# A hybrid decoder step on one core: q kept by feature in the delta rule, the output scaling put behind the next tile's masks, and the gate copy put ahead of the weight rounding

## The chip, the cores and the metric

The kernel runs on one core of one Trainium2 chip. The metric is the time of one execution on the device in microseconds (us), given as the median of three runs. The engines are TensorE (PE; its weight loads are listed as PEld), VectorE (DVE), ScalarE (ACT), GpSimd (POOL), and SyncE (SP), which issues the transfers.

## The reference, cut to what matters

One decoder layer for a prompt of 2048 tokens (16 meta tokens before it) and 8 running sequences of 4 tokens, model width 1024. Window attention and a gated delta rule work side by side, are merged by sigmoid gates, and a feed-forward block follows. The part that the change touches is the delta rule: 4 heads of 128, chunks of 64 tokens.

```
qb = _l2norm(heads(qb, DK)) * (DK ** -0.5)
kb = _l2norm(heads(kb, DK))

def _gated_delta_chunk(S, q, k, v, g, beta):
    gc = jnp.cumsum(g, axis=-1)
    decay = where(incl, exp(gc[..., :, None] - gc[..., None, :]), 0.0)
    kk = einsum('bhid,bhjd->bhij', k, k)
    a_mat = where(strict, beta[..., :, None] * decay * kk, 0.0) + eye(L)
    eg = exp(gc)
    rhs = beta[..., None] * (v - eg[..., None] * (k @ S))
    u = triangular_solve(a_mat, rhs, lower=True, unit_diagonal=True)
    qk = einsum('bhid,bhjd->bhij', q, k) * decay
    o = eg[..., None] * (q @ S) + qk @ u
    S_new = exp(gc[..., -1]) * S + einsum('bhjd,bhj,bhje->bhde', k, exp(gc[..., -1:] - gc), u)

# behind it, for each token and head:
y = o * rsqrt(mean(o * o) + EPS) * w * silu(z)
```

## The kernel before

The prompt is worked in four groups of 512 tokens, each of four tiles of 128 tokens (two chunks each). Group 1 has a fifth, small tile "S" of 48 columns ahead of them: the meta tokens and the 8 running sequences. A group goes through projections, a short convolution (`conv`, which leaves q, k and v by feature in `post`), the delta rule tile by tile, the `z` projection, the output projections and the feed-forward block. Each engine has its own program (`tensor`, `scalar`, `gpsimd`, `vector`) in an order written out by hand; semaphores join them, and each queue is worked in its order.

A tile of the delta rule, by TensorE: `delta_rows` turns k, q and v from feature-major into rows (banks 6, 2, 7) and spreads the cumulated decays into bank 4; VectorE scales the rows (`scaled`: kn, qn, qe, kb, kw, bv); TensorE turns kn, qn and qe back (`turned`), ScalarE copies them (`turned_copy`) to kTd, qT and a part of WQ; `delta_scores` makes k k^T and k q^T; `delta_args` (VectorE) and `delta_decays` (ScalarE) make the decay masks, `delta_masks` applies them and leaves X; five levels of small products (`PT`, `DT`) invert the triangle; then WU (W transposed and U), and for each of the two chunks a product with the state S (L1390), u, the state's increment (L1402), the output (L1407) and the update of S (L2535). `row_squares`, `row_sums_of` and `row_factors` make the norms of the next tile's q and k; `delta_out` scales the output of the tile before.

In between, in numbered steps 0 to 17, `beside(t, k)` puts other work: quarters of the 16 gate products (`gate_quarter`, all in bank 0; in group 1 the last quarter of each gate is followed by 48-column products for the small tile) and the attention of the next tile (`attention_step`: inputs at step 2, scores at 3 and 8, softmax at 5 and 10, transposes at 6 and 11, values at 7 and 13). `QUARTERS` says how many quarters stand at each step; in groups 2 to 4 a gate ends at steps 2, 6, 12 and 17 of each tile. In group 1 a tile holds 11 quarters, so the ends fall elsewhere in each.

Weights come through SyncE's queue into `raw`; ScalarE rounds a unit (`weights_hi`, L617) and VectorE takes the rest (`weights_lo`, L624). A ring of three units holds both parts. When a gate j ends, `gate_logits` on ScalarE rounds the unit two ahead and then copies bank 0:

```
j = gate_k[0]
gate_k[0] += 1
hi_until("gate", j)
if first and j == 8:
    act.wait_ge(*made("state_out", 16))
act.wait_ge(*made("gate_ps", (j + 1) * (1 + F)))
...
act.copy(gate[:, j, MAIN], bank[0][:]).then_inc(sem("gate_e"), 1)
```

Of the kernel before, what the change touches and what calls it, by code (L numbers as in the profile page):

```python
# [59 lines left out]
assert sum(QUARTERS) * NT == 64 and QUARTERS_C + sum(QUARTERS_S) + sum(QUARTERS_0) * NT == 64  # L60
# [66 lines left out]
for _v, _names in {  # L127
# [28 lines left out]
            "osq_done rope_done",  # L156
# [23 lines left out]
            "bt_ps bt_rd nat_ps",  # L180
# [20 lines left out]
        (0, 30, 24):  # L201
# [7 lines left out]
        (0, 45, 36):  # L209
# [113 lines left out]
def program(nc, d):  # L323
# [422 lines left out]
    def group(g, first):  # L746
# [38 lines left out]
        quarters_of = lambda t: QUARTERS_S if t == "S" else QUARTERS_0 if first else QUARTERS  # L785
# [96 lines left out]
        def tensor(pe, claim):  # L882
# [263 lines left out]
            def rows_from(t, b, blk, v):  # L1146

                n = n_of(t)
                claim(b, "natq_done", v)
# [4 lines left out]
            def delta_values(t):  # L1154

                rows_from(t, 7 if first or t else 2, 2, 6 * ix[t] + 6)

            def delta_rows(t):
# [3 lines left out]
                rows_from(t, 6, 1, 6 * i + 5)  # L1162
                rows_from(t, 2, 0, 6 * i + 3)
                if first or t:
                    delta_values(t)
                claim(4, "arg_done", 2 * i + 2)
# [5 lines left out]
            def turned(t, q, b, src):  # L1172

                i, n = ix[t], n_of(t)
                pe.wait_ge(*made("natq_done", 6 * i + q + 1))
                claim(b, "bt_rd", 3 * i + q + 1)
                for x in range(NH):
                    last = nc.tensor.transpose(bank[b][:, n * x:n * (x + 1)], q4[src][0:n, x, :], c("ident")[0:n, 0:n])
                last.then_inc(sem("bt_ps"), 1)

            def delta_scores(t):

                i, w = ix[t], own_w(t)
                qT, kTd = q4["qT"], q4["kTd"]
                pe.wait_ge(*made("bt_rd", 3 * i + 1))
# [5 lines left out]
                pe.wait_ge(*made("bt_rd", 3 * i + 2))  # L1191
                claim(2, "QK_done", i + 1)
                for x in range(NH):
                    for cs in chunks(t):
                        last = nc.tensor.matmul(bank[2][cs, w * x:w * (x + 1)], kTd[:, x, cs], qT[:, x, cs], start=True, stop=True)
                last.then_inc(sem("kk_ps"), 1)

            def inside_conv(j):
# [7 lines left out]
                if not first and j == NCONV - 1:  # L1206
                    turned(0, 0, 1, "kn")
                    turned(0, 1, 3, "qn")
                    turned(0, 2, 5, "qe")
# [39 lines left out]
            def delta(t):  # L1249
                i, n, w = ix[t], n_of(t), own_w(t)  # L1250

                if first or t:
                    turned(t, 0, 1, "kn")
                    turned(t, 1, 3, "qn")
# [3 lines left out]
                if first or t:  # L1258
                    turned(t, 2, 5, "qe")
# [79 lines left out]
                if t == "S":  # L1339

                    pe.wait_ge(*made("WT_rd", 1))
                    pe.wait_ge(*made("bt_rd", 3))
                    claim(3, "small_done", 3)
                    for x in range(NH):
# [5 lines left out]
                        if x == 1:  # L1350
                            gate_quarter()
# [245 lines left out]
        def scalar(act):  # L1597
# [52 lines left out]
            def gate_logits():  # L1650
# [3 lines left out]
                hi_until("gate", j)  # L1654
# [52 lines left out]
            def turned_copy(t, q, b, dst):  # L1707

                n = n_of(t)
                act.wait_ge(*made("bt_ps", 3 * ix[t] + q + 1))  # L1710
                act.copy(WQ[:, :, CH:CH + n] if dst == "qeT" else q4[dst][:, :, 0:n], bank[b][:, 0:NH * n].rearrange("p (h n) -> p h n", h=NH)).then_inc(sem("bt_rd"), 1)

            def delta_decays(t):
# [6 lines left out]
                for x in range(NH):  # L1720
                    act.activation(q4["dA"][0:n, x, 0:w], q4["dA"][0:n, x, 0:w], ACT.Exp, scale=-1.0,
                                   bias=tg2[0:n, s, x:x + 1]).then_inc(sem("dec_done"), 1)
                for x in range(NH):
# [16 lines left out]
            for j in range(NCONV):  # L1740
# [4 lines left out]
                if not first and j == NCONV - 1:  # L1745
                    turned_copy(0, 0, 1, "kTd")
                    turned_copy(0, 1, 3, "qT")
# [1144 lines left out]
```

## Time and profile before

| what | value |
|---|---|
| median of three runs | 3335.37 us (3330.85 to 3346.25) |
| the profiled execution, its own time | 3332.55 us |
| its span, first to last instruction | 3330.7 us |
| mean granted TensorE clock | 0.990 |
| TensorE, VectorE, ScalarE, GpSimd busy | 97%, 60%, 46%, 12% of the span |
| delta rule of group 1, about | 162 to 453 us |

The page gives each engine's busy time; the timeline gives start, length, engine, line, operation, written and read tiles, a count where equal instructions are merged, and in brackets how long the engine had stood and what released it. The granted clock is 1.00 at full rate (2.4 GHz) and 0.50 at the lower level (1.2 GHz). Line numbers are those of the kernel before.

### The profile page before, as it was taken

How to read it: one execution, taken by the hardware profiler on the slowest of the kernel's cores; microseconds unless marked ns; L12 is line 12 of the kernel's file. 1: busy time of each engine (PE TensorE's matmuls, PEld its weight loads, DVE VectorE, ACT ScalarE, POOL GpSimd, SP SyncE). 2: the span in 40 equal slices, each digit the busy share in tenths (PEclk: the TensorE clock that was granted, in tenths of full speed). 3: DMA queues.
4: the chain of work that ended last, by engine and by line, in shares of the span. 5: the costliest groups of instructions: out<-in, count | busy, mean ns of one | idle time of the engine just before them, and what ended most of it. 6: DMA issues, size and time to landing. Idle time of an engine off the chain costs nothing. (4 is left out here: it accounts for less than half of the span.)

```text
span 3330.7 us, 59185 instructions
## 1 busy us (share of the span) xinstructions
PE 3247.1 (97%) x23574; PEld 2841.8 (85%) x23574; DVE 1986.5 (60%) x3721; ACT 1520.0 (46%) x3173; POOL 413.5 (12%) x453
## 2 busy tenths in 40 slices
PE   8999899999999999999999999999999999999998
PEld 7877789999998777898998777889998777789896
DVE  6645545543547654685766754587575855578484
ACT  5324443222235554464554654455454654446362
POOL 2211100432503111000003011000001211000000
PEclk9989999999999999999999999999999999999999
DMA  4211013655743111354553211345463211246463
GB/s 161 63 56 46 25 58 111 229 194 199 257 154 110 54 46 63 116 160 138 165 193 109 73 39 46 114 137 167 137 213 124 78 44 43 80 129 183 124 177 97
DMA packets 142816, 392.47 MB, mean 118 GB/s; under 512 B 18288, under 2 KB 20288, under 8 KB 139072
## 3 DMA queue, kind: packets, MB, share of 16 engines
q1 hardware_dynamic: 142544, 388.69, 36.5%
q8 instruction: 190, 3.11, 0.4%
q14 instruction: 82, 0.67, 0.1%
HBM read 353.95 MB, written 35.69 MB: 117 GB/s over the span
## 5 line engine op out<-in xcount | busy, mean ns | idle before, releaser
L624 DVE TENSOR_TENSOR wl<-raw,wh 128x512 fp32r<-128x512 f32 (+1 forms) x795 | 747.1, 947 | 573.2 <-ACT wh L617 569.6
L617 ACT CAST wh<-raw 128x512 fp32r<-128x512 f32 (+1 forms) x795 | 636.0, 808 | 459.6 <-PE bank L892 370.8
L892 PE MATMUL bank<-xnT,wh 128*128 128x512 f32 (+2 forms) x2432 | 725.3, 382 | 9.0 <-ACT gate L1663 7.3
L892 PE MATMUL bank<-hnT,wh 128*128 128x256 f32 (+2 forms) x3016 | 580.7, 290 | 3.1 <-ACT V L1959 3.1
L892 PEld LDWEIGHTS bank<-xnT,wh 128*128 128x128 f32 x2432 | 430.3, 192 | 81.6 <-issue 16.5
L892 PEld LDWEIGHTS bank<-hnT,wh 128*128 128x128 f32 x3016 | 473.6, 188 | 8.5 <-ACT V L1959 3.7
L892 PE MATMUL bank<-hid,wh 128*128 128x512 f32 (+1 forms) x1760 | 467.6, 353 | 0.0
L892 PE MATMUL bank<-xnT,wl 128*128 128x512 f32 (+2 forms) x1280 | 461.8, 365 | 0.0
L892 PE MATMUL bank<-hnT,wl 128*128 128x256 f32 (+2 forms) x1508 | 437.2, 290 | 0.0
L892 PE MATMUL bank<-Tm,wh 128*128 128x256 f32 x2016 | 368.7, 282 | 0.2 <-ACT sg L1959 0.2
L892 PEld LDWEIGHTS bank<-hid,wh 128*128 128x128 f32 x1760 | 309.5, 188 | 46.0 <-issue 0.3
L892 PEld LDWEIGHTS bank<-Tm,wh 128*128 128x128 f32 x2016 | 310.2, 189 | 1.0 <-ACT sg L1959 0.8
L892 PE MATMUL bank<-hid,wl 128*128 128x512 f32 (+1 forms) x880 | 311.0, 353 | 0.0
L892 PEld LDWEIGHTS bank<-hnT,wl 128*128 128x128 f32 x1508 | 283.6, 188 | 2.1
L892 PE MATMUL bank<-Tm,wl 128*128 128x256 f32 x1008 | 284.1, 282 | 0.0
L892 PEld LDWEIGHTS bank<-xnT,wl 128*128 128x128 f32 x1280 | 245.9, 192 | 41.2
L892 PEld LDWEIGHTS bank<-Tm,wl 128*128 128x128 f32 x1008 | 190.3, 189 | 0.0
L892 PEld LDWEIGHTS bank<-hid,wl 128*128 128x128 f32 x880 | 165.4, 188 | 23.8
L892 PE MATMUL bank<-mixT,wh 128*128 128x512 f32 (+1 forms) x640 | 170.7, 355 | 1.8 <-DVE mixT L2593 1.8
L892 PE MATMUL bank<-oT,wh 128*128 128x512 f32 (+1 forms) x640 | 169.5, 353 | 1.3 <-ACT sz L1897 1.3
L892 PEld LDWEIGHTS bank<-mixT,wh 128*128 128x128 f32 x640 | 113.9, 190 | 18.8 <-ACT mixT L1919 2.0
L2351 DVE SCALAR_TENSOR_TENSOR cy<-pre,pr,cy 128x512 f32<-128x512 f32 (+1 forms) x144 | 125.3, 870 | 5.1
(380 smaller groups left out, 4527.3 us busy)
## 6 DMA issues: line engine op xcount, KB each, us to landing
raw<-in_wstream SPq DMA_DIRECT2D x346, 512.0 KB, 3.5
raw<-wsum SPq DMA_DIRECT2D x252, 256.0 KB, 3.4
raw<-in_wstream SPq DMA_DIRECT2D x189, 256.0 KB, 2.8
ops_in<-in_wstream SPq DMA_DIRECT2D x44, 512.0 KB, 7.6
wsum<-ops_out SPq DMA_DIRECT2D x22, 1024.0 KB, 6.3
hT<-in_xT SPq DMA_DIRECT2D x4, 2048.0 KB, 8.9
out_yp_out<-hT SPq DMA_DIRECT2D x16, 512.0 KB, 3.0
xr<-in_x_prompt SPq DMA_DIRECT2D x12, 512.0 KB, 7.9
```

Source lines behind the costliest of these rows:

```text
L617: act.copy(hi_cell(n), raw_cell(n)).then_inc(sem("hi_done"), 1)
L624: nc.vector.tensor_tensor(lo_cell(n), raw_cell(n), hi_cell(n).bitcast(F32), ALU.subtract).then_inc(sem("lo_done"), 1)
L892: ins = nc.tensor.matmul(*a, **k)
L2351: ins = v_.scalar_tensor_tensor(out, src(i), w(i), out, ALU.mult, ALU.add)
```

## The change

q is no longer scaled as rows. The unscaled q stays by feature in `post`; the scores of q and k read it there, and the part of WQ for q is `post` times `eG`, the exponential of bank 4, which ScalarE makes in one instruction more (`dec_done` counts 10 a tile instead of 9). q's norm enters as a factor of the output instead: GpSimd multiplies the mean square by the square of the factor (slot 1 of `fac`) before the root and the root by the factor (slot 0) after it. q rows are still made for tiles 1 to 3, for their sums of squares. The norm's root for k is taken apart from the one for q.

The order changes as well. `delta_args` of the next tile stands at the end of a tile in every group; ScalarE does tile 0's `delta_decays` inside the small tile in group 1. `delta_out` of the tile before stands behind step 1. Rounding and subtraction of gate weights (`gate_weights`) come behind the gate copy, and at step 17 only behind the next tile's decays (ScalarE) and scaled rows (VectorE). In group 1 three quarters move out of the small tile: 12 a tile instead of 11 in tiles 0 to 2, one at step 17, so gates end at steps 2, 7 and 14.

```
-QUARTERS_S = (1, 1, 1, 1, 1, 1, 0, 0, 1, 0, 0, 0, 0, 1, 2, 6, 0, 0)
-QUARTERS_0 = (1, 1, 1, 0, 1, 1, 1, 1, 0, 1, 1, 0, 1, 0, 1, 0, 0, 0)
-S_FILL = (0, 3, 4, 6, 7, 8)
+QUARTERS_S = (1, 1, 1, 1, 1, 1, 0, 0, 1, 0, 0, 0, 0, 1, 1, 4, 0, 0)
+QUARTERS_0 = (1, 1, 1, 0, 1, 1, 1, 1, 0, 1, 1, 0, 1, 0, 1, 0, 0, 1)
+QUARTERS_E = (*QUARTERS_0[:17], 0)
+S_FILL = (2, 4, 6, 8)
...
+    eG = q4["qT"]
...
+        q_rows = lambda t: t not in ("S", 0)
...
                 rows_from(t, 6, 1, ...)
-                rows_from(t, 2, 0, 6 * i + 3)
+                if q_rows(t):
+                    rows_from(t, 2, 0, "sqc_done", 2 * NH + 2 * t)
...
-                        last = nc.tensor.matmul(bank[2][cs, ...], kTd[:, x, cs], qT[:, x, cs], start=True, stop=True)
+                        last = nc.tensor.matmul(bank[2][cs, ...], kTd[:, x, cs], q_of(x, cs), start=True, stop=True)
...
-                    turned(t, 0, 1, "kn")
-                    turned(t, 1, 3, "qn")
+                    turned(t)
...
-                    turned(t, 2, 5, "qe")
...
-                        if x == 1:
-                            gate_quarter()
...
+                    pe.wait_ge(*made("natq_done", 5 * i + 5))
...
 # ScalarE
-                hi_until("gate", j)
...
+                act.activation(eG[:, :, 0:n], bank[4][:, 0:NH * n]..., ACT.Exp).then_inc(sem("dec_done"), 1)
...
                     if quarters[0] % 4 == 0:
                         gate_logits()
+                        if k != 17:
+                            gate_weights()
...
+            def gate_weights():
+                if quarters[0] >= 4:
+                    hi_until("gate", quarters[0] // 4 - 1)
...
-                    turned_copy(t, 0, 1, "kTd")
-                    turned_copy(t, 1, 3, "qT")
-                    delta_decays(t)
+                    turned_copy(t)
+                    if t != 0:
+                        delta_decays(t)
+                    gate_weights()
                 beside(t, 0)
-                turned_copy(t, 2, 5, "qeT")
...
 # GpSimd
-                root(rr[0:n, 8:12], ss[0:n, 8:12], n, 1.0 / P, 4).then_inc(sem("orr_done"), 1)
+                link(nc.gpsimd.tensor_tensor(ss[0:n, 12:16], ss[0:n, 8:12], own(1), ALU.mult))
+                link(root(rr[0:n, 8:12], ss[0:n, 12:16], n, 1.0 / P, 4))
+                nc.gpsimd.tensor_tensor(rr[0:n, 8:12], rr[0:n, 8:12], own(0), ALU.mult).then_inc(sem("orr_done"), 1)
...
 # VectorE
+            def scaled_q(t):
+                dve.wait_ge(*made("dec_done", 10 * ix[t] + 6))
+                v_.tensor_tensor(WQ[:, :, CH:CH + n], post[:, 0:NH, col(t):col(t) + n], eG[:, :, 0:n], ALU.mult)...
...
-                    if quarters[0] % 4 == 0:
-                        lo_until("gate", quarters[0] // 4 - 1)
+                    if quarters[0] % 4 == 0 and k != 17:
+                        gate_weights()
...
-                if t == "S" or t and not first:
+                if t == "S":
                     delta_args(t)
-                if i:
-                    delta_out(tiles[i - 1])
                 beside(t, 0)
...
                     scaled(t, ("kb", "kw", "bv"))
+                    scaled_q(t)
+                    gate_weights()
...
                 beside(t, 1)
+                if i:
+                    delta_out(tiles[i - 1])
...
                         if k == 1 and t + 1 < NT:
                             delta_rows(t + 1)
-                        if first and k == 1 and t + 1 < NT:
                             delta_args(t + 1)
+                            sum_q(t + 1)
```

## Rows read from the trace of the kernel before

**Rows 1.** The page, part 1: busy us, share of the span, instructions.

```profile
PE 3247.1 (97%) x23574; PEld 2841.8 (85%) x23574; DVE 1986.5 (60%) x3721; ACT 1520.0 (46%) x3173; POOL 413.5 (12%) x453
```

**Rows 2.** TensorE's waits, whole span: us in total, times, longest.

```profile
PE bank L892 <- ACT gate L1663: 7.3, 13, 0.6
```

**Rows 3.** Timeline, group 4, seam into tile 3.

```profile
2809.86 1.04 ACT L617 CAST wh<-raw 128x1024 fp32r<-128x1024 f32 x1
2810.01 0.60 PE L1178 MATMUL bank<-cm,d_kn 128*128 128x128 f32 x4
...
2810.44 0.60 PE L1178 MATMUL bank<-cm,d_qn 128*128 128x128 f32 x4
2810.93 0.59 ACT L1663 COPY gate<-bank 128x512 f32<-128x512 f32 x1
...
2811.41 0.59 ACT L1711 COPY d_kTd<-bank 128x512 f32<-128x512 f32 x1
...
2811.66 0.70 PE L892 MATMUL bank<-xnT,wh 128*128 128x512 f32 x2 [0.62 <-ACT gate L1663]
...
2816.51 0.85 DVE L2340 TENSOR_TENSOR X<-cm,X 128x256 f32<-128x256 f32 x1
...
2817.68 0.68 PE L1268 MATMUL bank<-cm,X 64*64 64x64 f32 x16
```

**Rows 4.** Timeline, group 4, tile 2, step 2.

```profile
2768.82 1.05 ACT L617 CAST wh<-raw 128x1024 fp32r<-128x1024 f32 x1
...
2770.13 0.59 ACT L1663 COPY gate<-bank 128x512 f32<-128x512 f32 x1 [0.26 <-PE bank L892]
...
2771.77 1.13 PE L1088 MATMUL bank<-kT,qTt 64*128 64x256 f32 x8 [0.37 <-ACT kT L1680]
```

**Rows 5.** Timeline, group 4, tile 2, step 6.

```profile
2779.41 1.03 ACT L617 CAST wh<-raw 128x1024 fp32r<-128x1024 f32 x1
...
2780.57 1.23 DVE L624 TENSOR_TENSOR wl<-raw,wh 128x1024 fp32r<-128x1024 f32 x1 [1.06 <-ACT wh L617]
...
2782.00 0.66 DVE L2208 COPY pTm<-bank 128x512 f32<-128x512 f32 x1
...
2783.35 1.08 PE L1114 MATMUL bank<-pTm,vn 128*64 128x256 f32 x8
```

**Rows 6.** Timeline, group 1, seam into tile 1, and step 10.

```profile
295.70 0.66 PE L1178 MATMUL bank<-cm,d_kn 128*128 128x128 f32 x4 [1.90 <-DVE d_kn L2279]
...
297.22 1.05 PE L892 MATMUL bank<-xnT,wh 128*128 128x512 f32 x2
...
333.04 0.60 ACT L1663 COPY gate<-bank 128x512 f32<-128x512 f32 x1
...
335.74 1.97 PE L1100 MATMUL bank<-cm,sc 128*128 128x128 f32 x8 [2.17 <-ACT sc L1688]
```

**Rows 7.** Timeline, group 1, tile 3, step 14.

```profile
443.99 1.22 DVE L624 TENSOR_TENSOR wl<-raw,wh 128x1024 fp32r<-128x1024 f32 x1
...
446.38 0.20 ACT L1661 COPY gateS<-bank 128x48 f32<-128x48 f32 x1 [2.65 <-PE bank L892]
...
447.04 1.12 DVE L2535 SCALAR_TENSOR_TENSOR S<-S,egl,bank 128x128 f32<-128x128 f32 x4 [1.84 <-PE bank L1402]
```

**Rows 8.** Timeline, small tile: state product, and its seam.

```profile
205.06 1.20 PE L892 MATMUL bank<-xnT,wh 128*128 128x512 f32 x2
...
207.76 4.06 PE L1349 MATMUL bank<-d_WQ,Sb 128*128 128x8 f32 x32
...
246.11 1.03 PE L1178 MATMUL bank<-cm,d_qn 128*128 128x128 f32 x4 [0.72 <-DVE Sb L2515]
```

**Rows 9.** Windows: stretch, length, busy us by engine, granted clock, transfers.

```profile
191.00:192.00 1.00, 0.00 (x0) 0.00 (x0) 0.00 (x0) 0.96 (x4) 0.00 (x0) 1.00 0.00 0
...
293.80:295.70 1.90, 0.00 (x1) 0.01 (x1) 1.27 (x4) 1.75 (x7) 1.73 (x5) 1.00 0.00 0
297.20:300.70 3.50, 3.50 (x14) 2.92 (x13) 2.51 (x7) 2.14 (x9) 0.74 (x1) 0.53 0.00 0
```

More of the change, by code:

```diff
@@ L784, in group @@
         chunk_half = lambda x, k: k if x < NH // 2 else 1 - k
-        quarters_of = lambda t: QUARTERS_S if t == "S" else QUARTERS_0 if first else QUARTERS
+        quarters_of = lambda t: QUARTERS if not first else QUARTERS_S if t == "S" else QUARTERS_E if t == NT - 1 else QUARTERS_0
+        q_rows = lambda t: t not in ("S", 0)
+        nat_of = lambda t, k: sum(2 + q_rows(x) for x in tiles[:ix[t]]) + k
         def sync(sp):
@@ L1170, in delta_rows, with turned @@
                 last.then_inc(sem("G_ps"), 1)
-            def turned(t, q, b, src):
+            def turned(t):
                 i, n = ix[t], n_of(t)
-                pe.wait_ge(*made("natq_done", 6 * i + q + 1))
-                claim(b, "bt_rd", 3 * i + q + 1)
+                pe.wait_ge(*made("natq_done", 5 * i + 1))
+                claim(1, "bt_rd", i + 1)
                 for x in range(NH):
-                    last = nc.tensor.transpose(bank[b][:, n * x:n * (x + 1)], q4[src][0:n, x, :], c("ident")[0:n, 0:n])
+                    last = nc.tensor.transpose(bank[1][:, n * x:n * (x + 1)], q4["kn"][0:n, x, :], c("ident")[0:n, 0:n])
                 last.then_inc(sem("bt_ps"), 1)
@@ L1183, in delta_scores @@
                 i, w = ix[t], own_w(t)
-                qT, kTd = q4["qT"], q4["kTd"]
-                pe.wait_ge(*made("bt_rd", 3 * i + 1))
+                kTd = q4["kTd"]
+                q_of = lambda x, cs: post[:, x, col(t) + cs.start:col(t) + cs.stop]
+                pe.wait_ge(*made("bt_rd", i + 1))
                 claim(1, "A_done", i + 1)
@@ L1194, in delta_scores @@
                     for cs in chunks(t):
-                        last = nc.tensor.matmul(bank[2][cs, w * x:w * (x + 1)], kTd[:, x, cs], qT[:, x, cs], start=True, stop=True)
+                        last = nc.tensor.matmul(bank[2][cs, w * x:w * (x + 1)], kTd[:, x, cs], q_of(x, cs), start=True, stop=True)
                 last.then_inc(sem("kk_ps"), 1)
@@ L1341, in delta @@
                     pe.wait_ge(*made("WT_rd", 1))
-                    pe.wait_ge(*made("bt_rd", 3))
+                    pe.wait_ge(*made("natq_done", 5))
                     claim(3, "small_done", 3)
@@ L1789, in scalar @@
                 gate_logits()
+                hi_until("gate", 0)
             def beside(t, k):
@@ L2282, in delta_rows, with sum_k, sum_q @@
             def delta_rows(t):
[L2284 removed]
+                dve.wait_ge(*made("nat_ps", nat_of(t, 1)))
                 if ix[t]:
                     dve.wait_ge(*made("WU_ps", 2 * ix[t]))
[L2287 to L2290 removed]
+                if q_rows(t):
+                    dve.wait_ge(*made("rs_done", F + 2 * t))
                 scaled(t, ("kn",))
[L2292 to L2299 removed]
+            def scaled_q(t):
+                n = n_of(t)
+                dve.wait_ge(*made("dec_done", 10 * ix[t] + 6))
+                v_.tensor_tensor(WQ[:, :, CH:CH + n], post[:, 0:NH, col(t):col(t) + n], eG[:, :, 0:n], ALU.mult).then_inc(sem("natq_done"), 1)
+            def sum_k(t):
+                dve.wait_ge(*made("sqc_done", 2 * NH + 2 * t - 1))
+                v_.tensor_reduce(out=rs8[:, t + 1, NH:], in_=q4["kn"][:], op=ALU.add, axis=AX.X).then_inc(sem("sums_in"), 1)
+            def sum_q(t):
+                dve.wait_ge(*made("sqc_done", 2 * NH + 2 * t))
+                step(v_.tensor_reduce(out=rs8[:, t + 1, 0:2], in_=q4["qn"][:, 0:2], op=ALU.add, axis=AX.X))
+                for dst, src in HALVES:
+                    ins = v_.tensor_reduce(out=rs8[dst, t + 1, 2:NH], in_=q4["qn"][src, 2:], op=ALU.add, axis=AX.X)
+                    if dst.start == 0:
+                        step(ins)
+                ins.then_inc(sem("sums_in"), 1)
             def delta_args(t):
@@ L2367, in sums_copied @@
                 for n, sl in heads_of:
-                    v_.tensor_copy(rs8[0:n, sl, :], bank[6][0:n, 8 * sl.start:8 * sl.stop].rearrange("p (t h) -> p t h", h=8)).then_inc(sem("sums_in"), 1)
+                    sums = bank[6][0:n, 8 * sl.start:8 * sl.stop].rearrange("p (t h) -> p t h", h=8)
+                    if n == P:
+                        step(v_.tensor_copy(rs8[:, sl, 0:2], sums[:, :, 0:2]))
+                        for dst, src in HALVES:
+                            step(v_.tensor_copy(rs8[dst, sl, 2:NH], sums[src, :, 2:NH]))
+                        v_.tensor_copy(rs8[:, sl, NH:], sums[:, :, NH:]).then_inc(sem("sums_in"), 1)
+                    else:
+                        v_.tensor_copy(rs8[0:n, sl, :], sums).then_inc(sem("sums_in"), 1)
+                settle()
             for j in range(NCONV):
@@ L2450, in beside, with gate_weights @@
                     attention_step(after(t), IN_DELTA_S if t == "S" else IN_DELTA, k)
+            def gate_weights():
+                if quarters[0] >= 4:
+                    lo_until("gate", quarters[0] // 4 - 1)
             def delta_out(t):
```

94 lines of the change are left out of this document (45 added, 49 removed).

## The prediction

> **What bounds the kernel now.** The page first [rows 1]: TensorE is busy 97% of the span, VectorE 60%, ScalarE 46%. An edit pays only if it takes columns from TensorE, closes one of its gaps or keeps its clock up. Then the waits of TensorE [rows 2]: it stood 7.3 us in 13 places for the ScalarE copy that empties the one gate bank. Small sums, then, so everything hangs on whether gaps close or only move. I read the timeline at the places the diff touches: the seam between two tiles in group 4 [rows 3], the gate that finishes at step 2 and at step 6 of a tile [rows 4, 5], the seam and the last tile of group 1 [rows 6, 7], the small tile's state product [rows 8], and last the clock [rows 9].
>
> My sum is made against the profiled execution, 3332.55 us (span 3330.7); the runs shown have a median of 3335.37, so it stands 3 us below it. What this kernel's timing can tell from no change is about 0.5%, 17 us.
>
> **What leaves TensorE.** Four turned blocks of q cost 0.43 us (the first k block starts at 2810.01, the first q block at 2810.44) [rows 3]. Four row transposes of q have the same shape, and I take the same 0.43. The edit drops two turned groups (qn, qe) in each of 17 tiles and one group of q rows in five tiles (small tile, and tile 0 of four groups). That is 17 x 0.86 + 5 x 0.43 = 17 us if nothing stood in their shade; I spread it over the places below.
>
> *Seams in groups 2 to 4.* Now: k turned at 2810.01 (its weight loads at 2809.78), ScalarE rounds a weight unit first (2809.86), copies the gate at 2810.93, TensorE resumes at 2811.66 [rows 3]: 1.88 us from 2809.78. After: the copy starts where the rounding does now, 2809.9, and TensorE resumes as long after the copy's start as now, 0.73 us, so at 2810.6. Saved 1.04 us, qn inside it. The qe group goes, 0.43. X was late by about 0.3 us (it starts 2816.51, ready 2817.36; its user starts 2817.68) and is now early, since the arguments are written before the seam. About 1.7 us a seam, three seams in three groups: -15.3. VectorE loses two products and gains one; the added exponential (0.59 by the copies of that size) stands on ScalarE ahead of work that has 2 us of air. GpSimd's longer chain (a second root, two products, some 2 us) ends before the masks are wanted, which have 2 us of air as well. These I cost at nothing.
>
> *Tile 0 of groups 2 to 4*, inside the convolution: 0.86 + 0.43 = 1.3 us each, -3.9.
>
> **What the rounding costs where it lands.** Until now the rounding ran while ScalarE waited for the gate's last product: at step 2 it starts at 2768.82, the gate copy at 2770.13, and TensorE's scores wait only until 2771.77 [rows 4]. After the edit it comes behind that copy and ahead of the attention copies and the copies of PT and X, on an engine that takes its work in order. A rounding takes 1.05 us and holds the next instruction back 0.95, since one follows another 0.1 us before its end (copy 2810.93, 0.59 long, the next at 2811.41 [rows 3]). TensorE was already waiting there, so all of it shows: 4 tiles x 3 groups x 0.95 = +11.4.
>
> At step 6 VectorE's subtraction waits for the rounding. Now rounding 2779.41, subtraction 2780.57, second half of the turned probabilities 2782.00, TensorE uses them at 2783.35 [rows 5]. After: copy 2780.34, rounding 2780.82 to 2781.87, subtraction 2781.97, probabilities 2783.4 to 2784.05, use 2784.15: +0.8 in 9 tiles, +7.2. At step 12 the same shift is covered by two groups of products. Groups 2 to 4 so come to -15.3 - 3.9 + 11.4 + 7.2 = -0.6 us.
>
> **Group 1.** A seam there has no quarter to fill it: TensorE stands 1.9 us for kn, the first turned block starts 295.70, the next quarter 297.22 [rows 6]. After: a quarter fills it (1.4 us, taken from the small tile), kn is ready some 0.6 us before today's 295.7, as the root of k no longer waits for q, and only k is turned. Gone are 1.9 and 0.6 of waiting and 0.86 of q; X comes some 0.4 us later than TensorE wants it. -2.9 us x 3 = -8.7. Two of three seams are followed by the low clock, as by 0.53 over the 3.5 us from 297.2 [rows 9], which costs half of that: -3.2. The seam behind the small tile, 0.72 of waiting, two q groups and 3 us at low clock [rows 8]: -3.0. In the small tile: a quarter in the middle of the state product runs from 205.06 to 207.76, 2.7 us at the lower clock against 1.4 elsewhere [rows 8]: -1.35; its q groups and tile 0's rows -1.5; a weight unit no longer late, and its clock, -2, given back by 1.4 of a Y that is later. Behind 333.04 a gate finishing at step 10 puts its copies before the softmax; TensorE stands 2.17 us until 335.74 and runs slow for 6 us [rows 6]. With 12 quarters a tile no gate ends at step 10: -2.2 - 3.2. Sum of the gains -25.
>
> Against it: gates now end at steps 2, 7 and 14 of each of the four tiles. Step 2: +0.95 x 4 = 3.8. Step 14 is the sharpest. In the one tile where a gate ends there today, the subtraction starts 443.99, long before the gate is done, and VectorE updates the state at 447.04 [rows 7]. After the edit: gate copies from 446.38, rounding from 447.05 to 448.1, subtraction to 449.35, state update then: 2.3 us later, with the second state product queued behind it. In the other three 1.9, as attention rows fill a bit: +8.0. Step 7: 0.8 x 3 for the attention copy and 2.3 in the last tile, where no attention work stands in between: +4.7. The small tile's last products: +0.8. That is +17.3. Stalls of 1.9 us or more are often followed by the low clock and one of 1.5 is not [rows 9]; I take half of five at 1.6 us, +4. Group 1: -25 + 21.3 = -3.7.
>
> **Sum:** 3332.55 - 0.6 - 3.7 = 3328.2, I say 3328. The bounds of what the trace does not show: the subtraction and the rounding may fit wholly into waits (0 instead of 11.4 + 7.2 + 17.3 = 36 us) or cost 1.05 + 1.23 us at each end that no product group covers, 24 of the 48 inside a tile (55 us instead of the 29 taken for them, 3354). I take the values between, because the order of each queue is written out and each has been followed to its waiter. Added exponential and scaled q: between 0 and 0.6 us x 17.
>
> **Rivals.**
> *The roundings are hidden anyway.* TensorE's queue holds quarters and scores that could stand in for 0.9 us. For: only 0.37 us of wait shows before the scores today [rows 4]. Against: that wait shows that ScalarE is the last to come. Time: 3332.55 - 19.2 - 25 = 3288. If only step 2 or group 1's step 14 is hidden, 3308 to 3318.
>
> *Slower: every new stall takes the clock down.* One mechanism, at steps 2, 6 and 14: the stall before the scores and the values. Today a seam's 1.9 us is followed by 3.5 us at about 1.2 GHz [rows 9]; if the 21 stalls of 0.8 to 0.95 us in groups 2 to 4, added to the waits that stand there, do so too, they cost 21 x 1.7 = +36, group 1's other half +4: 3368 at the full price, 3348 at half. It decides from some ten such falls on. Against: the 1.5 us stall ahead of 192 left the clock at full [rows 9]. The Trainium skill, TensorE: Matmul & The Clock Gate, section "HAM oscillation", says that short gaps between groups of work can throttle the engine again and again, each return paid anew; by that rule this rival holds, at the price just given; the trace agrees for the long gaps only.
>
> *The first products wait for the arguments' new neighbours.* GpSimd's second root makes the masks late. Price 1 us x 16 = +16, 3344. Against: 2 us of air.
>
> *The reordering does nothing measurable and only the removed transposes count:* 3332.55 - 17 = 3316.
>
> **Chances.** Gains and roundings cancel (3318 to 3342): 0.45. Roundings hidden, wholly or partly, or only the transposes count: 0.37. Clock: 0.12. GpSimd late: 0.06. Faster by more than 0.5% (below about 3316): 0.35; within: 0.47; slower: 0.18. Range 3298 to 3348; the cancelling case alone 3318 to 3342.
>
> **What would show it.** Turned k starts at the seam in groups 2 to 4, with a gate quarter some 0.8 us behind it instead of 1.9. The scores of step 2 wait for kT some 1.3 us instead of 0.4, the values of step 6 for pTm, in group 1 the second state product for S some 2 us, four times. The waits for d_kn and d_qn are gone. TensorE loses 17 x 8 + 5 x 4 = 156 transposes. Wrong it is if the waits for kT stay at 0.4 or the clock of groups 2 to 4 leaves 1.00.

## The result and the profile after

The change made the kernel slower: a median of 3351.79 us (3346.28 to 3363.43, 15 runs) against 3339.52 us before (3329.38 to 3348.92, 15 runs), a ratio of 1.0036 with a 95% interval of 1.0023 to 1.0050. The forecast was 3328 us in a range of 3298 to 3348. The time lies 4 us above the range. The slowdown is small, but the interval is clear of 1, and it goes the other way than forecast: the forecast was made on an execution of 3332.55 us and so meant 4 us less; measured are 12 us more in the medians and 16 in the profiled executions. The outcome "within 0.5%", which had the most chance, came true, for another reason than the one given. The profiled execution took 3348.76 us (span 3346.8, granted clock 0.989), where the one before took 3332.55 (span 3330.7, 0.990).

The page's part 1 of the kernel after: busy us, share of the span, instructions.

```profile
PE 3235.3 (97%) x23418; PEld 2830.2 (85%) x23418; DVE 1986.3 (59%) x3740; ACT 1506.3 (45%) x3156; POOL 424.6 (13%) x511
```

TensorE lost the 156 transposes forecast and 11.8 us of busy time [rows 1], and yet the span grew by 16.1 us. So its idle time, what the span holds beside the busy time, grew by 28. TensorE's waits over the whole span (us in total, times, longest) say where:

```profile
PE bank L1094 <- ACT kT L1680: 13.8, 12, 1.3
...
PE bank L1120 <- issue: 10.2, 9, 1.1
...
PE bank L1391 <- DVE S L2578: 7.1, 4, 2.2
...
PE bank L1175 <- DVE qkv L2209: 4.3, 3, 1.5
PE bank L898 <- ACT gate L1663: 3.5, 10, 0.5
```

The gate copy went from 7.3 to 3.5 us [rows 2]. In its place stand scores that wait for kT, values (L1120, formerly L1114) that wait for turned probabilities, the second state product that waits for S, four times, and the spread of the decays (L1175, formerly L1168), which waits for attention rows. (For L1120 the view names no releaser, only "issue"; the timeline below shows it start 0.10 us behind the end of the copy of pTm.)

Lining up the two traces by the groups of products that both kernels have gives the balance. Where tile 0 of group 2 begins, the changed kernel is 1.7 us late; at the end of group 4's delta rule it is 16.5 us late. Groups 2 to 4 carry 14.7 us of the 16.1. The 1.7 us hide more: at 150 us, ahead of all that the change moved in group 1, the changed kernel is 1.9 us early, because the trace before has one low stretch of the clock more there (from 116.5 us, 6.8 us long); at the end of group 1's delta rule (453 us in the trace before) it is 3.2 us late, so that stretch alone cost 5.1; and another low stretch of the trace before (from 536.3 us) gives 1.5 back. In groups 2 to 4 the pattern repeats:

| place, groups 2 to 4 | forecast | measured |
|---|---|---|
| seam, turned k to scores | -1.04 | -0.72 |
| seam, scores to X | -0.43 - 0.3 | -0.39 |
| step 2, scores behind kT (tiles 1 and 2); products behind the copies of PT and X (tiles 0 and 3) | +0.95 | +0.88 to 0.96 |
| step 6, values behind pTm | +0.8 | +1.20 |
| tile 0, inside the convolution | -1.3 | -0.33 |

The seam into tile 3 of group 4, timeline:

```profile
2826.48 0.60 PE L1185 MATMUL bank<-cm,d_kn 128*128 128x128 f32 x4
2826.68 0.58 ACT L1663 COPY gate<-bank 128x512 f32<-128x512 f32 x1 [0.26 <-PE bank L898]
...
2827.41 0.70 PE L898 MATMUL bank<-xnT,wh 128*128 128x512 f32 x2 [0.33 <-ACT gate L1663]
...
2831.13 0.42 DVE L2366 TENSOR_TENSOR X<-cm,X 128x256 f32<-128x256 f32 x1
...
2833.03 0.68 PE L1270 MATMUL bank<-cm,X 64*64 64x64 f32 x16
```

Against [rows 3]: the gate copy starts 0.20 us behind the turned k's start instead of 0.92, and the quarter follows 0.93 behind it instead of 1.65. X is ready at 2831.55, 1.5 us before it is used, and the first product with it still starts 0.33 us behind the start of the quarter's last product, as it did before: that X was "late by 0.3" was a misreading.

Step 2 and step 6 of tile 2 in group 4:

```profile
2784.52 0.59 ACT L1663 COPY gate<-bank 128x512 f32<-128x512 f32 x1 [1.21 <-PE bank L898]
...
2785.00 1.05 ACT L621 CAST wh<-raw 128x1024 fp32r<-128x1024 f32 x1
...
2786.62 0.28 ACT L1680 COPY kT<-bank 128x128 f32<-128x128 f32 x1
...
2787.04 1.14 PE L1094 MATMUL bank<-kT,qTt 64*128 64x256 f32 x8 [1.26 <-ACT kT L1680]
```

```profile
2795.74 0.58 ACT L1663 COPY gate<-bank 128x512 f32<-128x512 f32 x1 [0.93 <-PE bank L898]
2796.22 1.05 ACT L621 CAST wh<-raw 128x1024 fp32r<-128x1024 f32 x1
...
2797.07 0.74 POOL L2073 TENSOR_TENSOR d_m<-d_dA,cm 128x256 f32<-128x256 f32 x1 [4.26 <-PE bank L1296]
...
2797.40 1.50 DVE L628 TENSOR_TENSOR wl<-raw,wh 128x1024 fp32r<-128x1024 f32 x1 [2.56 <-ACT wh L621]
...
2799.10 0.66 DVE L2223 COPY pTm<-bank 128x512 f32<-128x512 f32 x1
...
2799.86 1.08 PE L1120 MATMUL bank<-pTm,vn 128*64 128x256 f32 x8 [1.13 <-issue]
```

Against [rows 4, 5]: the rounding (CAST) now stands between the gate copy and the copy of kT, and TensorE waits 1.26 us instead of 0.37. At step 6 the subtraction, which waits for the rounding, starts 1.66 us behind the gate copy's start, and takes 1.50 us instead of 1.23. It starts while GpSimd's product (2797.07, 0.74 us) is running. At step 12 nothing was lost, as forecast.

Group 1: step 14 of tile 0, where the state update (L2578) stands behind the subtraction on VectorE, and step 7 of tile 3, where the products of Y wait for two small subtractions behind it:

```profile
281.98 1.07 ACT L621 CAST wh<-raw 128x1024 fp32r<-128x1024 f32 x1
...
283.08 1.23 DVE L628 TENSOR_TENSOR wl<-raw,wh 128x1024 fp32r<-128x1024 f32 x1 [4.06 <-ACT wh L621]
...
284.55 1.11 DVE L2578 SCALAR_TENSOR_TENSOR S<-S,egl,bank 128x128 f32<-128x128 f32 x4
...
285.04 2.05 PE L1391 MATMUL bank<-S,d_WQ 128*128 128x128 f32 x8 [1.64 <-DVE S L2578]
```

```profile
426.04 1.07 ACT L621 CAST wh<-raw 128x1024 fp32r<-128x1024 f32 x1
427.23 1.22 DVE L628 TENSOR_TENSOR wl<-raw,wh 128x1024 fp32r<-128x1024 f32 x1 [6.80 <-ACT wh L621]
428.38 0.28 DVE L2531 TENSOR_TENSOR Y<-Y,bank 128x128 f32<-128x128 f32 x1
...
428.95 0.71 PE L1296 MATMUL bank<-Y,d_m 64*64 64x64 f32 x16 [3.23 <-issue]
```

Tile 0 of group 2, where VectorE's attention rows (L2209) hold up the spread of the decays:

```profile
1105.04 1.22 DVE L628 TENSOR_TENSOR wl<-raw,wh 128x1024 fp32r<-128x1024 f32 x1
1106.17 0.42 DVE L2209 TENSOR_TENSOR qkv<-bank,st 128x256 f32<-128x256 f32 x1
...
1106.65 1.16 PE L1175 MATMUL bank<-cm,gt 128*128 128x128 f32 x8 [1.40 <-DVE qkv L2209]
```

And the clock, two windows of group 3 (stretch, length, busy us by engine, granted clock, transfers), with the wait of tile 3's step 2 that stands ahead of the second one. Before, the clock stayed at 1.00 in groups 2 to 4; each of these falls is 3.4 us at the lower level and costs 1.5 to 1.7 us:

```profile
2058.88 0.46 PE L1322 MATMUL bank<-PT,X 64*64 64x64 f32 x16 [1.56 <-ACT X L1840]
```

```profile
1905.00:1910.00 5.00, 4.96 (x31) 3.61 (x32) 3.12 (x15) 0.63 (x2) 0.00 (x0) 0.66 0.37 108
2059.00:2064.00 5.00, 5.00 (x40) 3.74 (x43) 0.87 (x3) 0.00 (x0) 0.00 (x0) 0.66 0.39 133
```

Four traces have the rounding behind the copy at step 2 of groups 2 to 4: this one and those of experiments 2, 4 and 8 below. They have 11 such falls, and not just anywhere: 9 come 0.4 to 1.1 us after the start of the product that ended tile 3's wait of 1.56 us (12 such waits; 0.62 us before), 2 come 2.1 and 2.6 us after tile 0's scores, which had waited 0.82 us (12 such). None follows the 24 waits of 1.26 us in tiles 1 and 2, nor those at step 6.

### The profile page after: what moved, and what is told of

Its sections match the earlier page's. It is cut to its first block and busy times, and to the rows that moved or that the text cites. A ratio compares the mean times of both kernels' runs of the same rounds, so it can differ in the third digit from the quotient of the medians.

```text
span 3346.8 us, 58927 instructions
## 1 busy us (share of the span) xinstructions
PE 3235.3 (97%) x23418; PEld 2830.2 (85%) x23418; DVE 1986.3 (59%) x3740; ACT 1506.3 (45%) x3156; POOL 424.6 (13%) x511
## 5 line engine op out<-in xcount | busy, mean ns | idle before, releaser
L898 PEld LDWEIGHTS bank<-mixT,wh 128*128 128x128 f32 x640 | 112.8, 188 | 18.7 <-ACT mixT L1927 2.0
L898 PEld LDWEIGHTS bank<-oT,wh 128*128 128x128 f32 x640 | 112.5, 188 | 18.4 <-issue 2.0
```

The lines of the kernel that those rows point to most:

```text
L898: ins = nc.tensor.matmul(*a, **k)
```

## The experiments

Ratios are to executions of the kernel before that ran beside each kernel (medians of 3337.3 to 3342.3 us); n counts a kernel's own executions. Executions of one kernel differ mostly in how long the clock is low, and that mostly in group 1: the traces of kernels 1, 6, 9 and 10, which have one program there, lost 27.3 us to the clock in their first 1000 us, three times, and 18.8 once. So the table also has the part that differs less: span times granted clock, median over a kernel's executions, roughly the span that would be left had the clock never been low (the clock is given to 0.001, so each is good to about 2 us; for the kernel before, it was 3297.2 to 3297.7 each time). What the clock took is the rest of the span.

| kernel | n | median us | ratio (95%) | span x clock | rest |
|---|---|---|---|---|---|
| before | 15 | 3339.5 | 1 | 3297.5 | 40 |
| after | 15 | 3351.8 | 1.0036 (1.0023 to 1.0050) | 3307.9 | 43.5 |
| 1: after, rounding first inside a tile | 6 | 3297.7 | 0.9883 (0.9855 to 0.9911) | 3274.9 | 20 |
| 2: before, rounding behind inside a tile | 6 | 3384.2 | 1.0136 (1.0104 to 1.0167) | 3326.1 | 56 |
| 4: after, rounding first at step 6 of groups 2 to 4 | 12 | 3340.8 | 1.0012 (0.9994 to 1.0031) | 3298.3 | 40 |
| 5: before, gate copy first at the seams | 10 | 3330.1 | 0.9977 (0.9961 to 0.9993) | 3290.6 | 37 |
| 6: as 1, k turned twice at the seams | 4 | 3302.6 | 0.9889 (0.9864 to 0.9914) | 3274.3 | 26 |
| 7: as 1, group 1's quarters as before | 6 | 3310.8 | 0.9914 (0.9892 to 0.9936) | 3280.3 | 26.5 |
| 8: after, rounding first in group 1 | 12 | 3336.3 | 0.9976 (0.9959 to 0.9993) | 3297.3 | 37 |
| 9: as 1, attention rows ahead of the subtraction | 6 | 3300.2 | 0.9885 (0.9864 to 0.9905) | 3270.1 | 28 |
| 10: as 1, rounding first at the seams too | 4 | 3308.6 | 0.9905 (0.9875 to 0.9934) | 3279.9 | 26.5 |

The theory after the result: the rounding behind the gate copy, inside a tile, costs more than everything else gains; and at the seam it is the order that gains, not the transposes. The rivals: the waits belong to something else that the change moved (the exponential, the scaled q), or only come together with it.

**1. Rounding first inside a tile** (the changed kernel, ScalarE):

```
                     if quarters[0] % 4 == 0:
+                        if k != 17:
+                            gate_weights()
                         gate_logits()
-                        if k != 17:
-                            gate_weights()
```

> The changed kernel with one thing undone: inside a tile ScalarE rounds a gate's weights before it copies the gate, as it did before the change; only the seam keeps the new order. Theory (the rounding behind the gate copy is what made the change slower): groups 2 to 4 give back 0.9 us in each of 12 tiles at step 2 and 1.2 us in each of 12 at step 6, about 25 us, and group 1 about 8 to 12 at steps 2, 7 and 14, so 33 to 37 us below the changed kernel and some 20 below the kernel before (3315 to 3320 where that one stands at 3339). Rival (the roundings only use a wait that something else would need anyway, such as the exponential or the scaled q): the waits for kT and pTm stay, and at most 10 us come back.

Measured: 1.5% below the changed kernel, 54 us in the medians, of which 33 are in span times clock, as much as was expected in all, and the rest clock, which was not expected. Groups 2 to 4 gave back 26 us in the trace where about 25 were expected, and that is partly luck: it is 0.9 at each of 12 steps 2, 1.2 at step 6 in nine tiles and not twelve (tile 3 has no next tile whose values could wait there), 0.5 more at step 2 of each tile 0, and the two falls of the clock. Step 2 and step 6 of tile 2 in group 4:

```profile
2746.61 1.06 ACT L621 CAST wh<-raw 128x1024 fp32r<-128x1024 f32 x1
...
2747.92 0.59 ACT L1663 COPY gate<-bank 128x512 f32<-128x512 f32 x1 [0.26 <-PE bank L898]
...
2749.56 1.13 PE L1094 MATMUL bank<-kT,qTt 64*128 64x256 f32 x8 [0.37 <-ACT kT L1680]
...
2758.39 1.23 DVE L628 TENSOR_TENSOR wl<-raw,wh 128x1024 fp32r<-128x1024 f32 x1 [1.04 <-ACT wh L621]
...
2761.18 1.08 PE L1120 MATMUL bank<-pTm,vn 128*64 128x256 f32 x8
```

The wait for kT is 0.37 us again and the values don't wait. The rival is out.

**2. The mirror: the kernel before, rounding behind inside a tile.**

```
                     if quarters[0] % 4 == 0:
-                        gate_logits()
+                        gate_logits(k == 17)      # rounds ahead of the copy only at 17
+                        hi_until("gate", quarters[0] // 4 - 1)
...
-            def gate_logits():
+            def gate_logits(ahead=True):
...
-                hi_until("gate", j)
+                if ahead:
+                    hi_until("gate", j)
```

> The kernel before with one thing changed: inside a tile ScalarE rounds a gate's weights behind the gate copy; the seams stay as they were. Theory (this order alone costs what the change lost): 12 x (0.9 + 1.2) = 25 us in groups 2 to 4, and some 5 in group 1, so 25 to 30 us slower than the kernel before, with waits for kT of 1.3 us and for the second half of pTm of 1.1 us as in the changed kernel. Rival (it costs only together with the change's other moves): less than 10 us slower.

```profile
PE bank L1114 <- issue: 11.3, 10, 1.1
...
PE bank L1088 <- ACT kT L1681: 11.1, 12, 1.3
```

Span times clock rose by 28.6 us, within the expected 25 to 30, with waits of the same kinds and sizes (total, times, longest); as in experiment 1, step 6 counts in nine tiles and not in twelve, so groups 2 to 4 make less of it (some 22 us) and group 1 more. The median rose by 45: 16 more went to the clock, mostly in group 1, whose granted clock over 160 to 480 us was 0.87 instead of 0.94. The order alone costs what the change lost, without any of the change's other moves. The rival (less than 10 us) is out.

**3. The kernel before with four copies of the sums.**

```
-                    v_.tensor_copy(rs8[0:n, sl, :], bank[6][0:n, 8 * sl.start:8 * sl.stop].rearrange("p (t h) -> p t h", h=8)).then_inc(sem("sums_in"), 1)
+                    sums = bank[6][0:n, 8 * sl.start:8 * sl.stop].rearrange("p (t h) -> p t h", h=8)
+                    if n == P:
+                        step(v_.tensor_copy(rs8[:, sl, 0:2], sums[:, :, 0:2]))
+                        for half in HALVES[0]:
+                            step(v_.tensor_copy(rs8[half, sl, 2:NH], sums[half, :, 2:NH]))
+                        v_.tensor_copy(rs8[:, sl, NH:], sums[:, :, NH:]).then_inc(sem("sums_in"), 1)
...
+                settle()
```

> The kernel before with the sums of squares in groups 2 to 4 copied by four VectorE instructions instead of one, as the changed kernel has it, and the same values. Theory (three instructions more, about 0.56 us, make TensorE's wait for the values of tile 0 longer by as much): the wait ahead of the spread of the decays (0.44 us before, 1.40 after the change) grows to about 1.0 us, 0.56 x 3 = 1.7 us in all. Rival (VectorE is late there for another reason): the wait stays at 0.44.

```profile
1102.51 1.16 PE L1168 MATMUL bank<-cm,gt 128*128 128x128 f32 x8 [0.84 <-DVE qkv L2194]
```

One execution, 3331.56 us, whose trace is what counts. The wait in the bracket is 0.84 us, against 0.44 before and 1.40 in the changed kernel: here three copies are worth 0.40 of the 0.96, less than the 0.56 expected. In the changed kernel two of them go from one half of the rows to the other, and the traces show the whole block of copies 0.56 us longer there than before (from its start to the next instruction 0.64 us instead of 0.08, in this experiment 0.51). The other part is the four q transposes that left TensorE ahead of that wait (0.44 us): VectorE was the last to come before the change too, so they were in its shade, and TensorE now waits for as long as it used to work. 0.56 and 0.44 make 1.00 of the 0.96; the second part follows from the traces and was not tested alone.

**4. Rounding first at step 6 of groups 2 to 4 alone.**

```
                     if quarters[0] % 4 == 0:
+                        if not first and k == 6:
+                            gate_weights()
                         gate_logits()
```

> The changed kernel with the old order (rounding, then gate copy) at step 6 of groups 2 to 4 alone. Theory: 12 x 1.2 = 14.4 us less than the changed kernel, and the subtraction there takes 1.23 us again instead of 1.50, because it no longer lies beside GpSimd's product. Rival (only the rounding's own shift of 0.8 is gone, the longer subtraction stays): 9.6 us less.

```profile
2787.18 1.23 DVE L628 TENSOR_TENSOR wl<-raw,wh 128x1024 fp32r<-128x1024 f32 x1 [1.06 <-ACT wh L621]
...
2788.37 0.74 POOL L2075 TENSOR_TENSOR d_m<-d_dA,cm 128x256 f32<-128x256 f32 x1 [4.26 <-PE bank L1296]
...
2789.96 1.08 PE L1120 MATMUL bank<-pTm,vn 128*64 128x256 f32 x8
```

The subtraction takes 1.23 us again and starts ahead of GpSimd's product; the values don't wait. Each step 6 gave back 1.20 us in the trace. With nine such places, not 12, the expected 14.4 should have been 10.8; span times clock fell by 9.6, which can't part the two sizes; that the subtraction is short again and each place gives 1.20 us back speaks against the rival.

**5. The kernel before with the gate copy first at the seams.** ScalarE:

```
-                        gate_logits()
+                        gate_logits(k != 17)      # at 17 no rounding in front
...
                     delta_decays(t)
+                    if not first:
+                        hi_until("gate", quarters[0] // 4 - 1)
```

and VectorE's subtraction of that unit moved from step 17 to behind `scaled(t, ("kb", "kw", "bv"))` of the next tile.

> The kernel before with the seam's order alone changed in groups 2 to 4: ScalarE copies the gate that ends at step 17 first and rounds behind the decays, VectorE subtracts behind the scaled rows; q is still scaled and turned. Theory (the 0.72 us that the changed seam saves between the turned k and the scores come from the gate copy's earlier start alone, and the turned q of that place lies in its shade): the same 0.7 us in each of 9 seams, 6.5 us in all, with the quarter 0.93 us behind the turned k instead of 1.65. Rival (the removal of the turned q is what saves them): the quarter comes 1.3 us behind, 0.3 us a seam, 2.7 in all.

```profile
2804.50 0.60 PE L1178 MATMUL bank<-cm,d_kn 128*128 128x128 f32 x4
...
2804.70 0.58 ACT L1664 COPY gate<-bank 128x512 f32<-128x512 f32 x1 [0.25 <-PE bank L892]
...
2804.94 0.60 PE L1178 MATMUL bank<-cm,d_qn 128*128 128x128 f32 x4
...
2805.43 0.70 PE L892 MATMUL bank<-xnT,wh 128*128 128x512 f32 x2
```

**6. k turned twice at the seams** (on kernel 1):

```
-                for x in range(NH):
+                for x in range(NH) if first or not t else (*range(NH), *range(NH)):
                     last = nc.tensor.transpose(bank[1][:, n * x:n * (x + 1)], q4["kn"][0:n, x, :], c("ident")[0:n, 0:n])
```

> The kernel of the first experiment (rounding first inside a tile) with the four transposes of the turned k done twice at the 9 seams of groups 2 to 4, the second time over the first. Theory (four transposes there lie in the shade of the gate copy): the next quarter starts as late behind the first turned k as without them (0.93 us), and the time stays within 1 us. Rival (every removed group was worth its 0.43 us): 0.43 us a seam, 3.9 us slower.

```profile
2778.82 1.04 PE L1185 MATMUL bank<-cm,d_kn 128*128 128x128 f32 x8
...
2779.75 0.71 PE L898 MATMUL bank<-xnT,wh 128*128 128x512 f32 x2
```

**10. Rounding first at the seams too** (on kernel 1):

```
                     if quarters[0] % 4 == 0:
-                        if k != 17:
-                            gate_weights()
+                        gate_weights()
                         gate_logits()
```

> The kernel of the first experiment with ScalarE's rounding in front of the gate copy at the seam too, so everywhere, as before the change; q stays by feature and unturned. Theory (at the seam the removed turned q saved nothing, the order saved it all): the quarter is again 1.65 us behind the turned k, 0.7 us a seam and 6.5 us in all slower than the first experiment. Rival (the missing four transposes are worth their 0.43 us there): 1.2 us behind, 0.3 a seam, 2.7 in all.

```profile
2792.12 0.60 PE L1185 MATMUL bank<-cm,d_kn 128*128 128x128 f32 x4
...
2793.76 0.70 PE L898 MATMUL bank<-xnT,wh 128*128 128x512 f32 x2 [1.05 <-ACT gate L1663]
```

These three belong together. With k and q turned (5) the quarter stands 0.93 us behind the turned k's start, with k turned twice (6) 0.93, with k alone but the rounding in front (10) 1.64. The seams of kernel 5 are each 0.72 us shorter than before, those of kernel 6 are equal to those of kernel 1 to 0.01 us, those of kernel 10 each 0.72 longer. So the group qn at the seam was worth nothing, and the order 6.5 us: span times clock moved by -6.9, -0.6 and +5.0. The median of kernel 6 is 5 us above kernel 1's, not within the expected 1 us, and its rest column is 6 above.

**7. Group 1's quarters as before** (on kernel 1):

```
-QUARTERS_S = (1, 1, 1, 1, 1, 1, 0, 0, 1, 0, 0, 0, 0, 1, 1, 4, 0, 0)
-QUARTERS_0 = (1, 1, 1, 0, 1, 1, 1, 1, 0, 1, 1, 0, 1, 0, 1, 0, 0, 1)
-S_FILL = (2, 4, 6, 8)
+QUARTERS_S = (1, 1, 1, 1, 1, 1, 0, 0, 1, 0, 0, 0, 0, 1, 2, 6, 0, 0)
+QUARTERS_0 = (1, 1, 1, 0, 1, 1, 1, 1, 0, 1, 1, 0, 1, 0, 1, 0, 0, 0)
+S_FILL = (0, 3, 4, 6, 7, 8)
...
+                        if x == 1:
+                            gate_quarter()
```

> The kernel of the first experiment with the gate quarters of group 1 where they stood before the change (11 a tile, none at a seam, one in the middle of the small tile's state product). Theory (the moved quarters are a gain of their own): three unfilled seams at some 1.5 us, the middle quarter 1.4, a gate ending at step 10 in front of the softmax 2.2, and the low clock behind such stalls 3 to 5, so 10 to 14 us slower than the first experiment. Rival (group 1's work is the same and the waits only move): within 4 us of it.

Measured: 13 us more in the median (0.3% by the ratios, 10 us), 5.4 in span times clock. The moved quarters are a gain of some 5 us of work, where about 8 were expected beside the clock; in the traces kernel 1 gains 4.6 us on kernel 7 between 150 and 453 us, though the clock takes 1.7 us more from it over 160 to 480 us. That they gain clock too isn't shown: the rest column of kernels 6, 9 and 10, whose group 1 is that of kernel 1, is 26 to 28, as this kernel's 26.5, and its trace lost less to the clock in its first 1000 us (22.2) than kernel 1's (27.3).

**8. Rounding first in group 1 alone** (on the changed kernel):

```
                     if quarters[0] % 4 == 0:
+                        if first and k != 17:
+                            gate_weights()
                         gate_logits()
```

> The changed kernel with the old order inside a tile (rounding, then gate copy) in group 1 alone. Theory (group 1's roundings behind the copy cost 14 us of stalls and as much again in clock where they take it down): 14 us less in the trace and 20 to 28 less in the median than the changed kernel. Rival (groups 2 to 4 carry the loss, whose order stays new here): at most 8 us less.

Measured: 15.5 us less in the median (0.6% by the ratios, 20 us), 10.6 in span times clock. In the trace group 1 gave back 20.5 us: 0.91 to 0.94 at each of four steps 2, 1.3 to 2.2 at each of four steps 14 (6.9 together), 2.8 of the stall at step 7 of tile 3, and the rest, some 7 us, clock. The stalls are 13.4 of them, as expected (14); over 160 to 480 us the clock was granted at 0.96 instead of 0.92. The median's gain is below the expected 20 to 28.

**9. Attention rows ahead of the weight subtraction** (on kernel 1, VectorE, convolution of groups 2 to 4):

```
+                if not first and j == NCONV - 2:
+                    attention_rows(0, 1)
                 lo_until("conv", j)
...
                 if not first and j == NCONV - 2:
-                    attention_rows(0, 1)
```

> The kernel of the first experiment, and in the convolution of groups 2 to 4 VectorE makes the attention rows (the tile that TensorE waits for ahead of the spread of the decays of tile 0, 1.4 us) before it subtracts the weights instead of behind that. Theory (the wait is the subtraction's 1.2 us and the three added copies, nothing else): the wait goes down by 1.1 to 1.2 us in three groups, 3.5 us in all, which the trace shows and the median hardly. Rival (the weights are then late for the next quarter): the stall moves a few products on and the span stays.

```profile
1090.93 0.42 DVE L2209 TENSOR_TENSOR qkv<-bank,st 128x256 f32<-128x256 f32 x1
1091.27 1.21 DVE L628 TENSOR_TENSOR wl<-raw,wh 128x1024 fp32r<-128x1024 f32 x1
...
1091.40 1.16 PE L1175 MATMUL bank<-cm,gt 128*128 128x128 f32 x8 [0.26 <-DVE qkv L2209]
```

The wait is 0.26 us instead of 1.4, three times; 4.3 us of waits went to 0.9, and span times clock fell by 4.8. The median (3300.2 against 3297.7) can't tell it: executions of both kernels fall at a clock of 0.990 or of 0.993 to 0.995. At 0.990 kernel 1 took 3307.9 and 3309.7 us and kernel 9 3303.2 to 3304.6; at 0.994 kernel 1 3296.4 and 3299.1 and kernel 9 3293.9. Both beat the kernel before by 1.2% (about 39 us in the medians, of which 23 and 27 in span times clock).

## Why the prediction was wrong

**What failed is the size of terms, not their kind.** The argument was that a saving at the seams and in group 1 would meet a cost at steps 2, 6, 7 and 14, and that they cancel. Each of these stalls came but one, behind the engine and the tile named (step 7 of tiles 0 to 2 stayed out), and one more came that had not been forecast, ahead of tile 0. In the traces the forecast was -4.3 us and +16.1 was measured. Of the 20.4 between, 15.3 stand in groups 2 to 4, forecast at -0.6 and measured at +14.7, and nearly all the rest in group 1, forecast at -3.7. The 15.3 are:

- *Seam, 9 x 0.59 = 5.3 us.* Three steps of its working failed. The copy was put "where the rounding does now, 2809.9", but the rounding needs no product and the copy does: the gate's last product ends only 0.2 us after the turned k's start, and the copy stands behind it. That is why 0.72 us were saved and not 1.04. X was taken as "late by about 0.3 us" because its user starts 0.32 us behind it [rows 3]; but that user starts just as close behind the quarter in front of it now that X is 1.5 us early. So its 0.3 us were never there to be saved. And qe was worth 0.39 of 0.43. In the sum qn stood inside the first saving and not beside it; experiments 5, 6 and 10 show that this saving was the order's alone.
- *Tile 0, 3 x 0.97 = 2.9 us.* The row transposes were counted at 0.43 us saved; they lay in the shade of a wait for VectorE, on which the edit put three more copies (experiment 3; experiment 9 takes the wait away). This cost was not in the sum at all.
- *Step 6, 9 x 0.4 = 3.6 us.* The new start of the subtraction was forecast within 0.1 us of what came, 1.6 us behind the gate copy's start. Its duration was taken from [rows 5], and moved in time it met GpSimd: 0.27 us of the 0.4 (experiment 4). Another 0.1 is the gate copy again: it was put at 2780.34, but in both traces it starts 0.20 us behind the next products' start, which is 2780.43 there.
- *Clock, 3.3 us.* It was taken to stay at 1.00, and fell twice. The prediction had named that as a sign of being wrong.

Together 15.1.

**Step 2** was right: +0.95 forecast, +0.88 to 0.96 measured, at all 16 tiles, though in tiles 0 and 3 not before the scores. **Group 1's costs** were right in sum by luck, 21.3 forecast and 20.5 measured (experiment 8), and partly wrong inside: step 14 came to 6.9 instead of 8.0, step 7 of tiles 0 to 2 to about 0.1 instead of 0.8 each, step 7 of tile 3 to 2.8 us instead of 2.3, and the clock took some 7 instead of 4. **Group 1's gains** are the other term that failed: forecast at 25 us, measured at 17.5 in the trace of experiment 8 between 150 and 453 us of the kernel before (18.7 at the end of the group, of which it had 1.3 before 150 us). The terms written down add up to 23.8 and not 25, as the 1.4 us of the later Y were left out. And more than 9 us of them were clock that would come back (seams, the small tile's product, step 10), of which the traces show 5.2: over 160 to 480 us the clock took 18.8 us before and 13.6 in experiment 8. Which of the places failed to give theirs back stays open. The upper bound has a slip as well: it says 29 us where the roundings' cost was 36 a sentence earlier; with 36 it is 3347 and not 3354.

**The rival of the hidden roundings** (3288) is refuted as a forecast, but its sum is tested by experiment 1, where the roundings really are hidden: it measured 0.9883, 39 us below the kernel before in the medians, where the gains alone had been put at 44. That this is near is luck. In the two traces, both at a clock of 0.990, it is 23.6 us: 11.3 in groups 2 to 4 instead of 19.2, and 12.9 in group 1 instead of 25. The rest of the medians' difference is the clock of other executions.

**The clock rival** held in part. Two falls followed in groups 2 to 4, not 21, so its price there was 3.3 us and not 18 to 36; the bound of ten falls was not reached. In group 1 it held more than forecast: some 7 us between the changed kernel's trace and experiment 8's, and in experiment 2 the rest column is 16 us above the kernel before. The Trainium skill, TensorE: Matmul & The Clock Gate, section "A second HAM failure mode: psum-queue depth-cycling", says of one kernel that its frequent short idle times between groups of products made the clock go down and up again and again. It is that section which bears on short gaps; "HAM oscillation", which the prediction names, tells of a kernel that waited for transfers between its groups. The traces agree in group 1, and in groups 2 to 4 for 11 waits in four traces, nearly all in tile 3. **GpSimd's longer chain** made no wait at the seam shown: its part for the output is done at 2832.26, and VectorE takes it up at 2835.37; the masks behind it are done at 2833.76, and TensorE takes them up at 2835.23. **Only the transposes count** (3316) is refuted: of the 17 us of turned and row transposes, at the seams of groups 2 to 4 the qn part (9 x 0.43) saved nothing, and the qe part 0.39 us of 0.43 each.

What stays open, beside the places in group 1: which of a kernel's executions get the low clock for longer. Kernel 1 lost 33 us to it in two executions and 17 to 20 in four, with the same program.

## What to carry to other kernels

When an instruction is moved behind another one on an in-order engine, ask what the engine did in that time before: if the instruction filled a wait for another engine, it was free there, and it can cost nearly its whole length wherever the queue behind it is awaited (0.9 of 1.05 us at step 2). Here one ScalarE and one VectorE instruction of 1.05 and 1.23 us, moved by one place, cost more than 156 removed transposes and a better order at the seams gained. Move such work only at the place where the copy is the one awaited (the seam), and keep it in front where it fills a wait. And a removed instruction saves its time only if it ends the wait in its place: four transposes ahead of a wait for another engine saved nothing at the seam and, as far as the traces tell, ahead of tile 0, and 0.39 of their 0.43 us where no such wait stood.

## What the runs showed of the hardware

VectorE's weight subtraction (128x1024) and GpSimd's product (128x256) held each other up. In the changed kernel's trace, where a product had started 0.11, 0.32 or 0.55 us ahead of the subtraction, the subtraction took 1.69, 1.50 or 1.26 us instead of 1.23, which is longer by what was left of the product (0.61, 0.42, 0.17 us) less 0.15, and the product kept its 0.73. In the trace before, where the subtraction had started 0.7 or 0.4 us ahead of the product, it kept its 1.23 us and the product took 1.11 or 1.41 instead of 0.73: the same sum with the parts changed over. In these places whichever starts first keeps its time and the other one pays, so a move of half a microsecond decides which of them is late. The Trainium skill, SBUF — State Buffer, section "Who interferes with whom", says that a VectorE instruction with two inputs in SBUF contends with a GpSimd instruction that reads SBUF, and that the order of issue decides which of them blocks. The traces agree; the prediction had not asked which of the two would now come first.
